# Hybrid trunk on one core: mixing attention in three batches of query blocks, and GpSimd for the parts of finished tiles

## What is computed

```python
s = jnp.einsum('bqhd,bkhd->bhqk', q_blk, k) * scale
s = jnp.where(kpos[None, :] <= qpos[:, None], s, NEG)
p = jax.nn.softmax(s, axis=-1)
return jnp.einsum('bhqk,bkhd->bqhd', p.astype(v.dtype), v)
...
y = jnp.concatenate([y_a, y_b, y_c], axis=-1) @ w_out[l]
```

## Time and profile before

| | us |
|---|---|
| median of 3 executions | 1677.78 (1677.75 to 1678.98) |
| profiled execution | 1677.16 |
| its span | 1675.3 |
| PE busy | 1593.8 (95%) |
| DVE busy | 911.5 (54%) |
| ACT busy | 732.6 (44%) |
| POOL busy | 1.3 (0%) |

### The profile page before, as it was taken

The page is one execution under the profiler, slowest core; times in us unless marked ns, Lnnn a source line. Parts: engine busy times, 40 slices in busy tenths (PEclk is TensorE's granted clock), DMA queues, the critical chain, the costliest instruction groups (busy, mean ns, idle before and its releaser), DMA issues.

```text
span 1675.3 us, 19235 instructions
## 1 busy us (share of the span) xinstructions
PE 1593.8 (95%) x7372; PEld 1239.3 (74%) x7372; DVE 911.5 (54%) x1418; ACT 732.6 (44%) x1246; POOL 1.3 (0%) x6
## 2 busy tenths in 40 slices
PE   7999999999999999999989989998999999999996
PEld 5775558877768888888767655687867788888884
DVE  5766655755375555532287666458354655555223
ACT  5544644535444444432245356455254444444221
POOL 0000000000000000000000000000000000000000
PEclk9999999999999999999999999999999999999998
DMA  6320004440213333333212200234303133333321
GB/s 229 113 76 26 1 1 151 151 126 26 88 51 91 100 100 102 100 113 101 88 48 91 89 13 1 76 101 164 113 13 101 51 101 101 101 101 101 107 69 51
DMA packets 38539, 143.48 MB, mean 86 GB/s; under 512 B 4272, under 2 KB 4400, under 8 KB 37936
## 3 DMA queue, kind: packets, MB, share of 16 engines
q1 hardware_dynamic: 38448, 142.25, 26.6%
HBM read 140.13 MB, written 2.10 MB: 85 GB/s over the span
## 4 chain that ended last, share of the span: by engine, by line
PE 87%; DVE 7%; ACT 3%; issue 3%; DMA 0%; SPq 0%; DVEq 0%; ACTq 0%
PE bank L530 25%; PE bank L532 24%; PE bank L531 24%; PE bank L782 2%; PE bank L882 2%; PE bank L810 2%; PE bank L872 1%; PE bank L798 1%; PE bank L722 1%; DVE x L1403 1%; DVE tn_x L1368 1%; PE bank L711 1%; PE bank L577 1%; DVE acc L1309 1%; DVE h_lo L1373 1%
## 5 line engine op out<-in xcount | busy, mean ns | idle before, releaser
L530 PE MATMUL bank<-h_hi,w_hi 128*128 128x512 f32 x1312 | 523.0, 399 | 26.2 <-DVE h_lo L1315 15.0
L1328 DVE TENSOR_TENSOR w_lo<-raw,w_hi 128x1024 fp32r<-128x1024 f32 x254 | 310.2, 1225 | 426.9 <-ACT w_hi L957 424.8
L532 PE MATMUL bank<-h_hi,w_lo 128*128 128x512 f32 x1312 | 513.0, 391 | 0.0
L531 PE MATMUL bank<-h_lo,w_hi 128*128 128x512 f32 x1312 | 512.8, 391 | 0.0
L957 ACT ACTIVATE w_hi<-raw 128x1024 fp32r<-128x1024 f32 x254 | 266.0, 1050 | 186.1 <-PE bank L532 175.8
L530 PEld LDWEIGHTS bank<-h_hi,w_hi 128*128 128x128 f32 x1312 | 247.6, 189 | 95.0 <-issue 24.3
L531 PEld LDWEIGHTS bank<-h_lo,w_hi 128*128 128x128 f32 x1312 | 247.8, 189 | 52.9 <-issue 2.9
L532 PEld LDWEIGHTS bank<-h_hi,w_lo 128*128 128x128 f32 x1312 | 247.5, 189 | 52.3
L530 PE MATMUL bank<-a_hi,w_hi 128*128 128x512 f32 x352 | 136.9, 389 | 0.0
L531 PE MATMUL bank<-a_lo,w_hi 128*128 128x512 f32 x352 | 136.9, 389 | 0.0
L532 PE MATMUL bank<-a_hi,w_lo 128*128 128x512 f32 x352 | 136.9, 389 | 0.0
(11 more groups left out here) (208 smaller groups left out, 1857.9 us busy)
## 6 DMA issues: line engine op xcount, KB each, us to landing
raw<-w_in SPq DMA_DIRECT2D x254, 512.0 KB, 3.6
x<-x_in SPq DMA_DIRECT2D x4, 512.0 KB, 7.5
mem<-mem_in SPq DMA_DIRECT2D x2, 1024.0 KB, 5.0
out<-x SPq DMA_DIRECT2D x4, 512.0 KB, 2.6
consts<-c_in SPq DMA_DIRECT2D x1, 1600.0 KB, 12.8
mem_sq<-mem_in SPq DMA_DIRECT2D x1, 1024.0 KB, 5.9
gains<-g_in SPq DMA_DIRECT2D x1, 80.0 KB, 3.5
```

The costliest lines, as they stand in the source:

```text
L530: pe.matmul(out_ap, l_hi, r_hi, start=start, stop=False)
L531: pe.matmul(out_ap, l_hi, r_lo, start=False, stop=False)
L532: return pe.matmul(out_ap, l_lo, r_hi, start=False, stop=stop)
L1328: dve.tensor_tensor(w_lo[:, s, :], raw[:, s, :], w_hi[:, s, :].bitcast(F32), ALU.subtract)\
```

## The change

The two changes are made together.

*Batches.* The four query blocks of a pair are taken in three batches (`BATCH`): blocks 0 and 1, block 2, block 3. A step c is one batch, 18 per layer. The scores of a batch lie side by side in one bank per head, its probabilities side by side in one slot. Each block still has its own score matmuls, mask and exponential; transposes and copies are made by batch: 3, 3 and 4 transposes per head, and one copy per head of 384, 384 and 512 columns. `pt_mix` is laid out by batch, in the order of `PLACES` (pairs of query block and key block), so the values become five matmuls per head, which read one to three runs of 128 columns. The lag stays two steps, six slots and four score banks stay.

*POOL.* For pairs 0 to 4 POOL makes high and low part. ACT makes the high part of pair 5 alone, DVE its low part. ACT waits for the low part of pair 4 first, and DVE's scale of a pair now waits for the low part of the pair two before.

```diff
+BATCH = ((0, 1), (2,), (3,))
+PLACES = (((1, 0), (1, 1), (0, 0)), tuple((2, k) for k in range(3)), tuple((3, k) for k in range(4)))
...
-            pt_mix = sb("pt_mix", [P, 2, TB, SEQ], F32, room)
+            pt_mix = sb("pt_mix", [P, 2, len(BATCH), SEQ], F32, room)
...
+        def batch_blocks(c):
+
+            pair, at = c // BATCHES, 0
+            for qb in BATCH[c % BATCHES]:
+                yield qb, at, 2 * (TB * pair + qb)
+                at += causal_len(qb)
+
+        def batch_end(c, i):
+
+            return 2 * (TB * (c // BATCHES) + BATCH[c % BATCHES][-1]) + i + 1
...
+                    for pair in range(MIX_PAIRS - 1):
+                        tile = mix_head(2 * pair)["tile"]
+                        pool.wait_ge(mix_scaled, count(mix_scaled, layer, pair + 1))
+                        pool.tensor_copy(h_hi[:, tile, :], sq[:, pair % 2, :]).then_inc(mix_at["out_hi"], 1)
+                        pool.wait_ge(mix_at["out_hi"], count(mix_at["out_hi"], layer, pair + 1))
+                        pool.tensor_tensor(h_lo[:, tile, :], sq[:, pair % 2, :], h_hi[:, tile, :].bitcast(F32), ALU.subtract)\
+                            .then_inc(mix_at["out_lo"], 1)
...
-                            if s == 1 and i == 0:
+                            if c == 1 and i == 0:
                                 wait_emptied(pe, layer, use_of("uv", TB - 1))
-                            if u >= 4:
-                                pe.wait_ge(mix_at["masked"], count(mix_at["masked"], layer, u - 3))
+                            if c >= 2:
+                                pe.wait_ge(mix_at["masked"], count(mix_at["masked"], layer, batch_end(c - 2, i)))
...
-                            pe.wait_ge(mix_at["exped"], count(mix_at["exped"], layer, u + 1))
-                            if s >= 1:
-                                pe.wait_ge(mix_copied[i], count(mix_copied[i], layer, s))
-                            for kb in range(s % TB + 1):
-                                mm = pe.transpose(turned[i][:, kb * P:(kb + 1) * P],
-                                                  pair_probs(u)[:, kb * P:(kb + 1) * P], const(C_IDENT))
+                            pe.wait_ge(mix_at["exped"], count(mix_at["exped"], layer, batch_end(c, i)))
+                            if c >= 1:
+                                pe.wait_ge(mix_copied[i], count(mix_copied[i], layer, c))
+                            first = {qb: at for qb, at, u in batch_blocks(c)}
+                            for n, (qb, kb) in enumerate(PLACES[c % BATCHES]):
+                                at = first[qb] + kb * P
+                                mm = pe.transpose(turned[i][:, n * P:(n + 1) * P], batch_probs(c, i)[:, at:at + P],
+                                                  const(C_IDENT))
                             mm.then_inc(mix_at["turned"], 1)
...
-                        for kb in range(TB):
+                        def values(kb, q0, rows, col, start, stop):
+
                             for i in range(2):
-                                mm = pe.matmul(outs[pair % 2][64 * i:64 * i + 64, kb * P:SEQ],
-                                               mix_head(2 * pair + i)["v"](kb), pt_mix[:, i, kb, kb * P:SEQ],
-                                               start=(kb == 0), stop=(kb == TB - 1))
-                        mm.then_inc(mix_at["out"], 1)
+                                mm = pe.matmul(outs[pair % 2][64 * i:64 * i + 64, q0 * P:(q0 + rows.stop - rows.start) * P],
+                                               mix_head(2 * pair + i)["v"](kb),
+                                               pt_mix[:, i, rows, col * P:(col + 1) * P], start=start, stop=stop)
+                            return mm
+
+                        values(0, 1, slice(0, 3), 0, True, False)
+                        values(1, 1, slice(0, 3), 1, False, False)
+                        values(2, 2, slice(1, 3), 2, False, False)
+                        values(3, 3, slice(2, 3), 3, False, True)
+                        values(0, 0, slice(0, 1), 2, True, True).then_inc(mix_at["out"], 1)
...
                     def pair_hi(pair):
 
+                        act.wait_ge(mix_at["out_lo"], count(mix_at["out_lo"], layer, pair))
...
-                        if t >= 1 and t % TB == 0:
-                            pair_hi(t // TB - 1)
+                        if t == PAIR_STEPS:
+                            pair_hi(MIX_PAIRS - 1)
...
-                            dve.wait_ge(mix_at["out_hi"], count(mix_at["out_hi"], layer, pair - 1))
+                            dve.wait_ge(mix_at["out_lo"], count(mix_at["out_lo"], layer, pair - 1))
...
+                    def pair_copy(c):
+
+                        n = len(PLACES[c % BATCHES]) * P
+                        dve.wait_ge(mix_at["turned"], count(mix_at["turned"], layer, 2 * c + 2))
+                        if c % BATCHES == 0 and c:
+                            dve.wait_ge(mix_at["out"], count(mix_at["out"], layer, c // BATCHES))
+                        dve.tensor_copy(pt_mix[:, 1, c % BATCHES, 0:n], turned[1][:, 0:n]).then_inc(mix_copied[1], 1)
...
-                        if t >= 2 and t % TB == 1:
-                            pair_lo(t // TB - 1)
+                        if t == PAIR_STEPS + 1:
+                            pair_lo(MIX_PAIRS - 1)
```

More of the change, by code:

```diff
@@ L473, in build, with batch_probs, score_bank @@
         MIX_PAIRS = MIX_HEADS // 2
[L474 to L483, removed]
+        BATCHES = len(BATCH)
+        PAIR_STEPS = MIX_PAIRS * BATCHES
+        def batch_probs(c, i):
+            at = (2 * c + i) % PAIR_PROBS
+            return p_mix[:, at, :] if at < PROBS else tn_mix[:, at - PROBS, :]
+        def batch_blocks(c):
[5 more added lines that the diff above has]
+            return 2 * (TB * (c // BATCHES) + BATCH[c % BATCHES][-1]) + i + 1
+        def score_bank(c, i):
+            return score_ring[(2 * c + i) % 4]
         with nc.Block() as block:
@@ L778, in pair_scores @@
+                        parts = [mix_head(2 * (c // BATCHES) + i)["parts"] for i in range(2)]
                         last = len(parts[0]) - 1
[L779 to L785, removed]
@@ L787, in pair_transposes @@
-                    def pair_transposes(s):
+                        for qb, at, u in batch_blocks(c):
+                            n = causal_len(qb)
+                            for part in range(last + 1):
+                                for i in range(2):
+                                    q, k = parts[i][part]
+                                    mm = pe.matmul(score_bank(c, i)[:, at:at + n], q[:, qb * P:n], k[:, 0:n],
+                                                   start=(part == 0), stop=(part == last))
+                                    if part == last:
+                                        mm.then_inc(mix_at["scored"], 1)
@@ L1204, in pair_exp @@
[L1204 to L1212, removed]
+                    def pair_copy(c):
+                        n = len(PLACES[c % BATCHES]) * P
+                        act.wait_ge(mix_at["turned"], count(mix_at["turned"], layer, 2 * c + 1))
+                        if c % BATCHES == 0 and c:
+                            act.wait_ge(mix_at["out"], count(mix_at["out"], layer, c // BATCHES))
+                        act.activation(pt_mix[:, 0, c % BATCHES, 0:n], turned[0][:, 0:n], ACT.Copy)\
+                           .then_inc(mix_copied[0], 1)
@@ new lines, in pair_exp @@
+                    def pair_exp(c):
+                        for qb, at, u0 in batch_blocks(c):
+                            n = causal_len(qb)
+                            for i in range(2):
+                                u = u0 + i
+                                act.wait_ge(mix_at["masked"], count(mix_at["masked"], layer, u + 1))
+                                p = batch_probs(c, i)[:, at:at + n]
+                                act.activation(p, p, ACT.Exp, scale=-1.0, bias=stat[:, 0, u:u + 1],
+                                               accum_out=stat[:, 1, u:u + 1]).then_inc(mix_at["exped"], 1)
@@ L1626, in pair_lo @@
                                                ALU.subtract), mix_at["out_lo"])
[L1628 to L1638, removed]
-                                -hd["scale"], 3e38, ALU.add, ALU.min, stat[:, 0, u:u + 1]), mix_at["masked"])
@@ L1641, in pair_copy, with pair_mask @@
-                    def pair_copy(s):
-                        qb, m = s % TB, s % TB + 1
-                        dve.wait_ge(mix_at["turned"], count(mix_at["turned"], layer, 2 * s + 2))
-                        if qb == 0 and s >= TB:
-                            dve.wait_ge(mix_at["out"], count(mix_at["out"], layer, s // TB))
-                        dve.tensor_copy(pt_mix[:, 1, 0:m, qb * P:(qb + 1) * P],
-                                        turned[1][:, 0:m * P].rearrange("p (b q) -> p b q", q=P))\
-                           .then_inc(mix_copied[1], 1)
+                    def pair_mask(c):
```

(14 more changed lines are left out.)

45 lines of the change are left out of this document (19 added, 26 removed).

## The result

The changed kernel takes 1666.49 us (median of 4, 1665.76 to 1666.65) for 1678.38 us before, measured beside it: a ratio of 0.9927, 95% interval 0.991 to 0.9945. Forecast were 1668.7 us and a range of 1664.5 to 1674.5. So ratios can be compared across experiments, and differences of 1 to 2 us between their medians can't.

The account below looks back on a forecast made before the run. PE was taken to bound latent pairs and DVE's chain window pairs; intervals summed to 73.3 and 73.2 us per stage (78.66 and 76.96 before), so 1677.8 - 9.1 = 1668.7 us, range 1664.5 to 1674.5.

Parts of the forecast that it names:

- Latent intervals: Between value matmuls of latent-head pairs, two per layer: PE's 0.46 us gap goes, 11.72 us becomes about 11.0.
- the rest of the third phase: Saving on PE in a latent interval, out of the 1.45 us third transpose phase: put at 0.10 us.
- The fifth value step: Value matmuls on PE, five steps for four: 0.05 us more per pair, values and spread 3.23 us.
- reading three runs: Value matmuls reading three runs of 128 columns instead of one of 384: between 0 and 0.5 us per pair, taken as 0.
- Window intervals: Between value matmuls of window-head pairs, two per layer: still DVE's chain (5.77 us), 9.8 us for 10.42.
- rival 4: Window pairs: nothing changes because ACT, its copy behind both exponentials of 512, becomes last; 1673 us, chance 0.08.
- Filling: Stage start to pair 0's values: DVE the chain after PE stands 1.7 us; values at 16.6 us, gain 1.0.
- Draining: Pair 4's values to pair 5's: 11.9 us, for 14.61 in layer 0 and some 13.1 in layer 1.
- POOL: POOL's copy and subtraction of 128x512 per pair: 0.6 and 1.2 us, hidden either way.
- Rival 1: DVE stands while POOL works, beside batch 0's masks: 1687 us, chance 0.07.
- rival 2: PE's clock falls elsewhere: if in both drains, +3.2 us, 1671.9 us; chance 0.22.
- Rival 3: New reads or value step cost 0.3 us on 12 pairs, 0.46 latent gap stays: +5.4, 1674 us; chance 0.12.

Follow-up runs that it names:

- reciprocal_late: Changed kernel with DVE's reciprocal of a pair moved from before the masks of block 2 to behind the copy of the last batch: 1664.78 us in one execution.
- batches_only: Changed kernel without POOL's work, ACT and DVE making high and low parts of every pair again: 1672.65 us, ratio 0.9951 to the kernel before.
- mlstm_low_late: Changed kernel with DVE's low part of the last mLSTM tile moved from its second step to its fifth: 1666.64 us, ratio 0.9928 to the kernel before.
- dve_two_inputs: Changed kernel with two unused 128x512 sums on DVE behind each scale, both inputs from SBUF: 1685.22 us in one execution.
- pool_only: Kernel before, its four steps per pair kept, with POOL making high and low parts of pairs 0 to 4: 1675.74 us, ratio 0.9977.

## Why the prediction was right, and where it was off

The direction, the mechanism and the range held; the size was 9.1 us for a measured 11.9 (12.15 in the stages of the profiled execution). By its own steps, per layer:

- *Latent intervals*, 11.0 forecast, 10.73 measured. The gap went, as said, and nothing took its place. The list of savings had a slip: by the earlier trace rows the rest of the third phase is 1.45 - 0.46 - 0.80 = 0.19 and not 0.10, with which it gives the 10.98 that PE's phases added up to. Two terms were mis-sized. The fifth value step costs nothing (0.05 taken): values and spread are 3.18 us before and after, and reading three runs costs nothing either, the term I had put between 0 and 0.5. And the scores of blocks 0 and 1 one behind the other take 1.51 us (202.24 to 203.75) for the 1.71 I added up from two phases; the transposes between them had cost PE something at both ends (the last matmuls of block 0 take 0.32 us before transposes and 0.23 before scores, the first of block 1 0.54 behind transposes and 0.43 behind scores). So the batches save PE 0.2 us on scores too, where the prediction had put 0.
- *Window intervals*, 9.8 forecast, 9.63 measured, DVE's chain 5.64 for 5.77. reciprocal_late (0.23 us off for 0.22) and batches_only (0.73 on for 0.71) show that it is the chain; rival 4 (ACT becomes last) is out.
- *Filling*, 16.6 forecast, 16.57 and 16.43 measured, with PE standing 2.05 us rather than 1.7: the three blocks' scores ahead of the stand were done 0.3 us sooner, and the masks came when they were expected. mlstm_low_late shows the chain.
- *Draining*, 11.9 forecast, 11.32 measured. The waits for ACT's copies were 0.35 and 0.82 us where I had put 0.5 and 1.1, and the eight transposes took 0.82 us up to the projection where I had put 1.02, their time up to scores; the drain of layer 1 before already had 0.82 (1064.49 to 1065.31).
- *POOL*, 0.6 and 1.2 us taken, 0.61 and 1.27 measured, hidden. Rival 1 is out: in dve_two_inputs the two engines held each other when DVE had two operands from SBUF, and in the changed kernel no mask or scale lengthened.
- *The clock*, rival 2. It fell in neither filling nor drain of the changed kernel in the profiled execution, where before it fell in both fillings and one drain. In the drain that is worth 1.5 us (14.61 against 13.07), which is part of layer 0's gain; the forecast had counted on it. Whether the change keeps the clock up there, or this was luck, isn't shown: batches_only fell in both drains, pool_only in neither, each in one profiled execution. In the filling the fall cost nothing before, as forecast. pool_only shows it, which fell in layer 0's filling and not in layer 1's. Here are the scores of block 2 of layer 1, before and in pool_only, the first at the lower clock:

```profile
999.66 1.65 PE L782 MATMUL bank<-k_nope,q_nope 64*128 64x384 f32 x4 [1.90 <-DVE stat L1637]
...
998.60 0.92 PE L790 MATMUL bank<-k_nope,q_nope 64*128 64x384 f32 x4 [1.90 <-DVE stat L1646]
```

Pair 0's values follow 15.56 us after the first score matmul in both. As a rival the clock was real: it took 3 us of batches_only and 2.6 of the 4.06 us that the stages of mlstm_low_late gave, these outside the stage, where I hadn't looked.
- *Rival 3* (new reads cost, latent gap stays) is out by the first point.

Summed: 73.3 and 73.2 us forecast for the stages, 71.8 and 71.7 measured. These 3.0 us are, in each layer, about 0.6 in the drain, 0.5 in the two latent intervals and 0.3 in the two window intervals. In the profiled execution the later start takes back 1.46 us, so it ended 10.7 us below the profiled one before; the rest of the medians' 11.9 can't be placed.

## What to carry to other kernels

In a pipeline of several engines, walk one period engine by engine from start-to-start times: the gain lies where the longest chain is, here PE's own phases in one kind of pair and DVE's list in the other, and the same edit is worth its full length in one and nothing in the other. Moving work off a chain can be as simple as changing its place in an engine's list: one instruction moved from DVE's second to its fifth step took 2 us off each stage, though the time of the whole kernel didn't show it. And two parts of a change need not add up: one can remove a wait that would have taken part of the other's gain. Before believing that a few microseconds are lost or won, compare the granted clock of stretches with the same work, also far from the edit.

## What the runs showed of the hardware

- A stand of PE of about 2 us may or may not be followed by some 3 us at 1.2 GHz: before, 2.04 us and the clock fell (0.57 from 173 to 177); after, 2.05 us in the filling too, and it didn't (1.00 over the whole stage); in layer 1 the stand was 1.90 us before and in pool_only, and the clock fell in the first alone. In the feed-forward part the same stand gave 0.86 over 12 us in one kernel and 1.00 in the other. Where PE was the chain a fall cost 1.3 to 1.5 us, and in the filling, where DVE was, nothing. So kernels that differ by one or two of them can differ by 0.1 to 0.2% without a difference in their work.
- POOL's copy of 128x512 with a cast takes 0.61 us and a subtraction 1.27, for 0.62 on ACT and 0.68 on DVE. They don't slow DVE instructions with one operand in PSUM; a DVE sum with both in SBUF went from 0.69 to 0.98 us, and POOL's copy and subtraction beside such sums from 0.61 to 1.13 and from 1.27 to 1.59.
- Value matmuls that read one to three runs of 128 columns run at the rate of those that read one run, and five pairs of them take no longer than four over the same columns.
